# Windowed attention of a hybrid encoder: the key tile beyond each end of a sequence is left out

## The chip, the cores and the metric

The kernel runs on 1 core of one Trainium2 chip. A core has five engines that run side by side and wait for each other by semaphores: TensorE (PE; its weight loads are listed as PEld), VectorE (DVE), ScalarE (ACT), GpSimd (POOL) and SyncE (SP), which here only issues transfers. Transfers run on 16 DMA engines that all queues share. The metric is the device time of one execution in microseconds.

## The reference, cut to what matters

Two token sequences, of 1024 and of 256 tokens, each get 16 meta tokens put in front and pass through one layer: an attention branch and a recurrent branch side by side, then a mixture of 32 experts. The attention is windowed: queries are taken in blocks of 128, and each block sees three blocks of keys, its own and the ones before and after, within a distance of 128, and the 16 meta keys:

```python
kpad = jnp.pad(kr, pad)                       # one block of zeros at either end
def band(n):
    qb = lax.dynamic_slice_in_dim(qr, n * ATTN_BLK, ATTN_BLK, axis=1)
    kb = lax.dynamic_slice_in_dim(kpad, n * ATTN_BLK, 3 * ATTN_BLK, axis=1)
    ...
    valid = (jnp.abs(ki - qi) <= WINDOW) & (ki >= 0) & (ki < s_len)
    s_win = jnp.where(valid, jnp.einsum('bqgrd,bkgd->bgrqk', qb, kb), -jnp.inf)
    s_met = jnp.einsum('bqgrd,bkgd->bgrqk', qb, km)
    return sink_softmax_av(s_win, vb, s_met, vm, sk)
```

For the first block of a sequence the block of keys before it does not exist, and for the last block the one after it: their scores are minus infinity for every query, and their probabilities are zero.

## The kernel before, in words

The two sequences lie one behind the other, 1280 tokens in NB = 10 blocks of 128. Blocks 0 to 7 are the first sequence, 8 and 9 the second. So blocks 0 and 8 are the first of a sequence, 7 and 9 the last.

`project` (from L162) normalises the tokens and makes the keys, values, queries and the recurrent branch feature tile by feature tile (products at L736, the recurrent gates at L758). Its POOL program (L332 to L363) writes zeros into two padding blocks of the key buffer in DRAM (L345 to L347), swaps rows of the keys for their rotation (L351), waits until the values are turned (L353), clears the two padding blocks of the token-major values in SBUF (L354 and L355) and stores the keys to DRAM (L357 to L363). ScalarE (L474) and POOL (L1193) wait for all key stores.

`mix` (from L801) is written as 12 steps, one per block and two to drain; a step is a hand-written order on each engine. Step t does attention for block t, the output product and residual of block t-1, and the router and list entries of block t-2 (`step` at L1383 on TensorE, L1539 on ScalarE, L1860 on VectorE; `run` at L1029 calls them with constant t).

- POOL: `window` (L1183) fetches the 384 keys of a block from DRAM to `k_win`, one of two buffers, one transfer for each of two key groups; `window(t + 1)` is issued at the start of POOL's step t. The 16 meta keys are fetched once into columns 384 to 400 of each buffer. `attn` (L1213) then waits for the exponentials and packs the meta probabilities.
- TensorE: `scores` (L1265) makes 8 heads of 128 x 400 scores, two products each (the high and low parts of the keys, both against the same stationary query parts), in two PSUM buffers that VectorE must have read two heads before. The heads are issued in four pairs among the output products (L1360) of block t-1, turns of block t-2 (L1324) and the router (L1338). `turn_probs` (L1281) turns each head's three 128 x 128 blocks of probabilities (L1288), in four pairs of heads, each behind six output products; a head waits until ScalarE has copied out the head two before. `times_v` (L1300) multiplies with the values: two 512-column instructions for the meta keys (L1307), then 8 heads x 3 key blocks, two instructions each (L1312).
- VectorE: `softmax_max` (L1647) scales, masks and writes one head of scores and takes its maximum (L1661); `rope_q` (L1600) rotates the query of the next block, `split_q` (L1640) splits it in a high and a low part, `attn_output` (L1838) makes the denominators and the attention output of the block before (L1853). The order in a step: attention output, heads 0 to 3, residual, heads 4 to 7, the router's choice of block t-2 (from L1689), rotation of the next query, two residuals, list places, split of the next query, scaled tokens of block t-1. In steps 0 and 1 splits of the output weights (L1637) stand in between.
- ScalarE: `exponentials` (L1439, one instruction per head at L1445), `probs_out` (L1458) copies the turned probabilities, three blocks per head, from PSUM (L1464), `sink_and_rec`, `meta_copy`, `q_split` (L1491).
- SP: swaps rows of the next query for its rotation (`swap_q`, L1066, four transfers at L1068), fetches masks and rotation tables (`tables`, L1058), tokens and weights.

The masks are made on the host (`layouts`, L2617): for a first block the first 128 columns are all minus infinity, for a last block columns 256 to 384.

After step 11, `plan` turns the counts of the router into a table of blocks of tokens per expert; `experts` (from L2006) reads the table and streams expert weights block by block.

Of the kernel before, what the change touches and what calls it, by code (L numbers as in the profile page):

```python
# [30 lines left out]
F32 = mybir.dt.float32  # L31
# [7 lines left out]
P = 128  # L39
D = 1024  # L40
META = 16
# [22 lines left out]
KEYS = WIN + META  # L64

# [96 lines left out]
def project(nc, sem, lasting_sem, block, mk, ps, a, feat, k_pre, v_tok, v_small, ident, eps_t, iota_e, list_dram, h2_dram, k_dram):  # L162
# [103 lines left out]
    v_padded = sem("v_padded")  # L266
    TILES_DONE = 2 * NCH + FTILES * NCH
    K_STORES = 16 * 18
# [63 lines left out]
    def _(pool):  # L332
# [11 lines left out]
        pool.wait_ge(fills, 3)  # L344
        for at in (META, META + P + REAL):  # L345
            pool.dma_start(k_dram[:, :, :, at:at + P].bitcast(F32), zeros[:, 0:4 * P].rearrange("p (g h c) -> p g h c", g=2, h=2)
                           ).then_inc(k_stored, 16)  # L347
# [5 lines left out]
        pool.wait_ge(v_turned, 1)  # L353
        for at in (0, (NB + 1) * P):  # L354
            pool.memset(v_tok[:, at:at + P], 0.0).then_inc(v_padded, 1)  # L355

# [359 lines left out]
    def _(pe):  # L716
# [68 lines left out]
        for k in range(FT):  # L785
            for d in range(2):
# [7 lines left out]
                k_cos_done=(k_cos_done, 1), k_swapped=(k_swapped, 16 * len(ROTATED)), v_out=(v_out, 2), v_padded=(v_padded, 2),  # L794
# [6 lines left out]
def mix(nc, ctx, sem, block, at, ps, a, projected, cleared_later, recycled, q_pre, rec, k_dram, v_tok, v_small, ident, eps_t, iota_e, counts, ix_x,  # L801
# [375 lines left out]
    def _(pool):  # L1177
# [5 lines left out]
        def window(t, s):  # L1183

            if not isinstance(t, int) or t >= 2:
                pool.wait_ge(scored, HEADS * t - HEADS)
                take_waits(pool)
            keys(s, slice(0, WIN), bass.ds(META + t * P, WIN), keys_in[s])
# [24 lines left out]
        def attn(t, s):  # L1213
            if has_next(t):
                window(t + 1, 1 - s)

            pool.wait_ge(exp_done, HEADS * t + HEADS)
            pool.wait_ge(meta_turned, t) if not isinstance(t, int) or t > 0 else None
            take_waits(pool)
            pool.tensor_copy(meta_p[:, :].rearrange("p (h m) -> p h m", m=META), probs[:, :, WIN:KEYS]).then_inc(meta_packed, 1)  # L1220
# [40 lines left out]
    def _(pe):  # L1261
# [3 lines left out]
        def scores(t, s, heads):  # L1265
            if heads[0] == 0:
                pe.wait_ge(q_lo_done, t + 2)
                if isinstance(t, int) and t == 0:
                    pe.wait_ge(projected["proj_out"], projected["PUT"])
                if isinstance(t, int) and t < RING:  # L1270
                    pe.wait_ge(k_meta_in[s], 32)
                pe.wait_ge(keys_in[s], 32 * (t // 2 + 1) if isinstance(t, int) else 16 * (t - s) + 32)
            for h in heads:

                pe.wait_ge(scaled, HEADS * t + h + 1)
                for part in range(2):
                    mm = pe.matmul(ps_sc[h % 2][:, 0:KEYS], q_parts[:, h, :], k_win[s][h // 4][:, part, :],  # L1277
                                   start=(part == 0), stop=(part == 1))
                mm.then_inc(scored, 1)

        def turn_probs(t, heads):  # L1281
            for h in heads:
# [4 lines left out]
                for j in range(3):  # L1287
# [12 lines left out]
        def times_v(t):  # L1300
            if isinstance(t, int) and t == 0:
                pe.wait_ge(v_meta_in, 16 * HEADS)
                pe.wait_ge(*projected["v_out"])
                pe.wait_ge(*projected["v_padded"])
# [3 lines left out]
            for h in range(HEADS):  # L1308
                pe.wait_ge(pt_out, HEADS * t + h + 3)
                for j in range(3):  # L1310
                    last = h == HEADS - 1 and j == 2
# [126 lines left out]
    def _(act):  # L1438
        def exponentials(t, heads):  # L1439
# [4 lines left out]
            for h in heads:  # L1444
                act.activation(probs[:, h, :], probs[:, h, :], ACT.Exp, bias=nmax[:, h:h + 1],  # L1445
# [12 lines left out]
        def probs_out(t, heads):  # L1458
            for h in heads:
# [4 lines left out]
                act.activation(probs_t[:, h, :], ps_t[h % 2][:, 0:WIN], ACT.Copy).then_inc(pt_out, 1)  # L1464
# [125 lines left out]
    def _(dve):  # L1590
# [56 lines left out]
        def softmax_max(t, s, heads, ahead_of_third=None):  # L1647

            for h in heads:
# [11 lines left out]
                dve.tensor_tensor_reduce(probs[:, h, :], ps_sc[h % 2][:, 0:KEYS], mask[s][:, :], HD ** -0.5, sink[:, h:h + 1],  # L1661
# [955 lines left out]
def layouts(i):  # L2617
# [37 lines left out]
    last = (SEQS[0] // P - 1, NB - 1)  # L2655
    first = (0, SEQS[0] // P)
    for b in range(NB):
        masks[b, :, 0:P] = NEG if b in first else np.where(kj >= qi, 0.0, NEG)
        masks[b, :, 2 * P:3 * P] = NEG if b in last else np.where(kj <= qi, 0.0, NEG)
# [39 lines left out]
```

## Time and profile before

| | |
|---|---|
| runs | 1231.37, 1232.2 and 1234.94 us; median 1232.2 us |
| profiled execution, first to last instruction (span) | 1231.0 us; the profile gives no other time for this execution |
| instructions | 21274 |
| TensorE busy | 1177.3 us, 96% of the span |
| VectorE busy | 926.7 us, 75% |
| ScalarE busy | 848.3 us, 69% |
| POOL busy | 253.0 us, 21% |
| mean granted TensorE clock | 0.992 |
| projections and recurrent branch | to about 257 us |
| attention steps 0 to 9 (value products end) | 257 to 529.6 us |
| drain, plan, table of blocks | to about 567 us |
| experts and final norm | to 1231 us |

The profile is one execution, taken by the hardware profiler. Busy time of TensorE is modelled, as its products are pipelined. The chain of waits goes back from the last instruction, at each step to what released it. A line of a view names the line of the kernel, the engine, what is written and read, and, behind a bar or in brackets, the idle time before it with what ended it.

### The profile page before, as it was taken

Reading aid. Unit: us, or ns where it says so; the run is one execution under the profiler, and the core shown is the slowest. Engines: PE = TensorE matmul, PEld = TensorE weight load, DVE = VectorE, ACT = ScalarE, POOL = GpSimd, SP = SyncE. Lnnn points to the kernel's source line nnn. Section 1 sums busy time; section 2 is a strip of 40 time slices with the busy share of each in tenths; the row PEclk is TensorE's granted clock in tenths of the full one; section 3 lists DMA queues with packets and bytes.
Section 4 is the critical chain, followed back from the end, with each engine's and each line's share of the span. In section 5 each row is a group of like instructions: output and inputs, shape, how many; then the busy total and the mean of one; then the engine's idle time right before and its main releaser. Section 6 shows DMA issues by size and latency. Waiting matters only on the chain.

```text
span 1231.0 us, 21274 instructions
## 1 busy us (share of the span) xinstructions
PE 1177.3 (96%) x6126; PEld 1007.2 (82%) x6126; DVE 926.7 (75%) x1214; ACT 848.3 (69%) x1042; POOL 253.0 (21%) x262
## 2 busy tenths in 40 slices
PE   5999999988999999999999999999999999999984
PEld 5999999977888888887788888888888888888872
DVE  5657887457777777758898867555888888888876
ACT  5538889567566666646777756555778777877775
POOL 2130000010111111012333213222322322322420
PEclk9999999999999999999999999999999999999997
DMA  7241110363233323346999987878999999999988
GB/s 289 89 127 40 43 44 29 83 183 95 87 114 93 107 91 91 120 173 246 389 393 404 382 271 254 322 250 315 393 380 384 395 378 377 390 373 373 401 304 334
DMA packets 67687, 295.60 MB, mean 240 GB/s; under 512 B 12469, under 2 KB 23094, under 8 KB 43058
## 3 DMA queue, kind: packets, MB, share of 16 engines
q1 hardware_dynamic: 48626, 252.63, 52.3%
q0 software_dynamic: 19008, 42.31, 14.1%
q8 instruction: 28, 0.46, 0.1%
q14 instruction: 25, 0.20, 0.0%
HBM read 263.98 MB, written 38.14 MB: 245 GB/s over the span
## 4 chain that ended last, share of the span: by engine, by line
PE 65%; DMA 20%; DVE 7%; ACT 4%; issue 3%; SPq 1%; POOL 0%; DVEq 0%; ACTq 0%; POOLq 0%
PE ps L2294 16%; PE ps L736 16%; DMA raw_w_gate<-in_w_gate 15%; PE ps L1360 8%; PE ps L2342 8%; PE ps L1312 4%; PE ps L758 2%; DVE g_lo L2499 2%; PE ps L1277 2%; ACT g_hi L2392 2%; PE ps L1288 2%; DMA raw_w_up<-in_w_up 2%; PE ps L1338 1%; PE ps L2281 1%; DMA z_a<-h_dram,ix_a 1%
## 5 line engine op out<-in xcount | busy, mean ns | idle before, releaser
L2499 DVE TENSOR_TENSOR g_lo<-raw_w_gate,g_hi 128x2048 fp32r<-128x2048 f32 x64 | 145.2, 2289 | 41.3 <-ACT g_hi L2392 41.1
L2499 DVE TENSOR_TENSOR d_lo<-raw_w_down,d_hi 128x2048 fp32r<-128x2048 f32 x62 | 140.5, 2289 | 44.5 <-ACT d_hi L2392 44.5
L2499 DVE TENSOR_TENSOR u_lo<-raw_w_up,u_hi 128x2048 fp32r<-128x2048 f32 x64 | 144.1, 2286 | 5.6 <-ACT u_hi L2392 5.2
L2392 ACT ACTIVATE g_hi<-raw_w_gate 128x2048 fp32r<-128x2048 f32 x64 | 120.9, 1913 | 37.6 <-DMA raw_w_gate<-in_w_gate 32.1
L2392 ACT ACTIVATE u_hi<-raw_w_up 128x2048 fp32r<-128x2048 f32 x64 | 120.9, 1913 | 17.3 <-DMA raw_w_up<-in_w_up 17.1
L736 PE MATMUL ps<-h_hi,w_hi 128*128 128x432 f32 (+2 forms) x368 | 127.6, 347 | 0.6 <-DVE w_lo L581 0.6
L736 PE MATMUL ps<-h_lo,w_hi 128*128 128x432 f32 (+2 forms) x368 | 126.3, 343 | 0.0
L736 PE MATMUL ps<-h_hi,w_lo 128*128 128x432 f32 (+2 forms) x368 | 126.1, 343 | 0.0
L2392 ACT ACTIVATE d_hi<-raw_w_down 128x2048 fp32r<-128x2048 f32 x62 | 116.8, 1909 | 13.5 <-DMA raw_w_down<-in_w_down 13.5
L2342 PE MATMUL ps<-d_hi,hid_hi 128*128 128x512 f32 x272 | 111.5, 410 | 0.7 <-DVE hid_lo L2528 0.7
L2342 PE MATMUL ps<-d_lo,hid_hi 128*128 128x512 f32 x272 | 107.3, 395 | 0.0
L2342 PE MATMUL ps<-d_hi,hid_lo 128*128 128x512 f32 x272 | 107.0, 393 | 0.0
L2222 POOL DMA_INDIRECT h_dram<-y_sb,ix_y x33 | 63.1, 1911 | 99.1 <-ACT y_sb L2428 93.9
L2294 PE MATMUL ps<-g_hi,ex_hi 128*128 128x512 f32 x272 | 75.1, 398 | 4.4 <-DVE ex_lo L2515 3.0
L2196 POOL COPY ix_x<-lists 128x2 int32 x33 | 14.1, 428 | 305.2 <-PE ps L2281 300.4
L2294 PE MATMUL ps<-u_hi,ex_hi 128*128 128x512 f32 x272 | 76.8, 404 | 0.0
L2294 PE MATMUL ps<-g_lo,ex_hi 128*128 128x512 f32 x272 | 74.4, 395 | 0.1
L2294 PE MATMUL ps<-u_lo,ex_hi 128*128 128x512 f32 x272 | 74.4, 395 | 0.0
L2294 PE MATMUL ps<-u_hi,ex_lo 128*128 128x512 f32 x272 | 74.3, 394 | 0.0
L2294 PE MATMUL ps<-g_hi,ex_lo 128*128 128x512 f32 x272 | 74.2, 394 | 0.0
L1661 DVE CUSTOM_DVE_ANT_0 probs<-ps,mask,sink_bc 128x400 f32<-128x400 f32 x80 | 47.5, 631 | 34.7 <-PE ps L1277 33.0
L736 PEld LDWEIGHTS ps<-h_hi,w_hi 128*128 128x128 f32 x368 | 69.9, 190 | 3.0 <-DVE w_lo L581 0.8
(374 smaller groups left out, 2729.9 us busy)
## 6 DMA issues: line engine op xcount, KB each, us to landing
raw_w_gate<-in_w_gate SPq DMA_DIRECT2D x64, 1024.0 KB, 10.8
raw_w_up<-in_w_up SPq DMA_DIRECT2D x64, 1024.0 KB, 12.5
raw_w_down<-in_w_down SPq DMA_DIRECT2D x62, 1024.0 KB, 12.0
k_win<-k_dram POOLq DMA_DIRECT2D x20, 384.0 KB, 5.7
w_raw<-in_w_in SPq DMA_DIRECT2D x14, 512.0 KB, 4.0
xh<-in_x SPq DMA_DIRECT2D x10, 512.0 KB, 3.4
h_dram<-xh SPq DMA_DIRECT2D x10, 512.0 KB, 3.8
u_dram<-u SPq DMA_DIRECT2D x10, 512.0 KB, 4.9
```

The lines of the kernel that those rows point to most:

```text
L736: mm = pe.matmul(ps[:, bank, 0:cols.stop - cols.start], w[s][:, k, :], h[:, k, cols], start=(k == 0 and n == 0), stop=(k == KD - 1 and n = ...
L758: mm = pe.matmul(bank[:, c, 0:n], w[:, g, :], x[:, cols], start=(j == 0), stop=(j == 2))
L1277: mm = pe.matmul(ps_sc[h % 2][:, 0:KEYS], q_parts[:, h, :], k_win[s][h // 4][:, part, :], start=(part == 0), stop=(part == 1))
L1288: mm = pe.transpose(ps_t[h % 2][:, j * P:(j + 1) * P], probs[:, h, j * P:(j + 1) * P], ident[:, :])
L1312: mm = pe.matmul(ps_o[:, h * HD:(h + 1) * HD], probs_t[:, h, j * P:(j + 1) * P], v_tok[:, bass.ds(t * P + j * P + (h // 4) * HD, HD)], sta ...
L1360: mm = pe.matmul(ps_y[i][:, :], x[:, k, :], w[:, k0 + k, half(i)], start=(k == 0 and n == 0), stop=(k == FT - 1 and n == 2))
L1661: dve.tensor_tensor_reduce(probs[:, h, :], ps_sc[h % 2][:, 0:KEYS], mask[s][:, :], HD ** -0.5, sink[:, h:h + 1], ALU.add, ALU.max, smax[:, ...
L2222: pool.indirect_dma_start(h2_dram, bass.IndirectOffsetOnAxis(ap=ix_y[:, 0:1], axis=0), y[:, :], None, compute_op=ALU.add).then_inc(y_added ...
L2294: mm = pe.matmul(ps[:, :], xs[:, c * KG + k, :], w[c][:, k * FE:(k + 1) * FE], start=(c == 0 and k == 0 and j == 0), stop=(c == 1 and k == ...
L2342: mm = pe.matmul(ps_y[:, i, :], h[:, c * KDN + k, :], w[c][:, cols], start=(c == 0 and k == 0 and j == 0), stop=(c == 1 and k == KDN - 1 a ...
L2392: act.activation(hi[c][:, :], raw[c][:, :], ACT.Copy).then_inc(hi_done, 1)
L2499: dve.tensor_tensor(lo[c][:, :], raw[c][:, :], hi[c][:, :].bitcast(F32), ALU.subtract).then_inc(lo_done, 1)
```

## The change

In steps 0 and 8 the first of the three key blocks is left out, in steps 7 and 9 the last. Scores, the scaled and masked scores, and exponentials cover 272 instead of 400 columns there; turns, copies and value products two instead of three blocks; the key fetch 256 instead of 384 keys. So that the columns stay next to each other in steps 7 and 9, the meta keys and probabilities sit in columns 256 to 272 there: step 7 fetches the meta keys once more, behind its 256 keys, into the buffer that step 9 uses too. The padding blocks of keys and values are no longer cleared, and the waits for that go. The other six steps are as before.

```diff
+FIRSTS = (0, SEQS[0] // P)
+LASTS = (SEQS[0] // P - 1, NB - 1)
+def chunks(t):
+    return range(1 if t in FIRSTS else 0, 2 if t in LASTS else 3)
+def meta_at(t):
+    return 2 * P if t in LASTS else WIN
+def key_cols(t):
+    return slice(chunks(t)[0] * P, meta_at(t) + META)
...
-    K_STORES = 16 * 18
+    K_STORES = 16 * 16
...
-        pool.wait_ge(fills, 3)
-        for at in (META, META + P + REAL):
-            pool.dma_start(k_dram[:, :, :, at:at + P].bitcast(F32), zeros[:, 0:4 * P].rearrange("p (g h c) -> p g h c", g=2, h=2)
-                           ).then_inc(k_stored, 16)
...
-        pool.wait_ge(v_turned, 1)
-        for at in (0, (NB + 1) * P):
-            pool.memset(v_tok[:, at:at + P], 0.0).then_inc(v_padded, 1)
...
-            keys(s, slice(0, WIN), bass.ds(META + t * P, WIN), keys_in[s])
+            lo, hi = chunks(t)[0] * P, (chunks(t)[-1] + 1) * P
+            keys(s, slice(lo, hi), slice(META + t * P + lo, META + t * P + hi), keys_in[s])
+            if t == LASTS[0]:
+                keys(s, slice(meta_at(t), meta_at(t) + META), slice(0, META), keys_in[s])
...
-            pool.tensor_copy(meta_p[:, :].rearrange("p (h m) -> p h m", m=META), probs[:, :, WIN:KEYS]).then_inc(meta_packed, 1)
+            pool.tensor_copy(meta_p[:, :].rearrange("p (h m) -> p h m", m=META), probs[:, :, meta_at(t):meta_at(t) + META]
+                             ).then_inc(meta_packed, 1)
...
-                pe.wait_ge(keys_in[s], 32 * (t // 2 + 1) if isinstance(t, int) else 16 * (t - s) + 32)
+                pe.wait_ge(keys_in[s], 32 * (t // 2 + 1) + (32 if t >= LASTS[0] and s == LASTS[0] % RING else 0))
...
-                    mm = pe.matmul(ps_sc[h % 2][:, 0:KEYS], q_parts[:, h, :], k_win[s][h // 4][:, part, :],
+                    mm = pe.matmul(ps_sc[h % 2][:, key_cols(t)], q_parts[:, h, :], k_win[s][h // 4][:, part, key_cols(t)],
...
-                for j in range(3):
+                for j in chunks(t):
                     mm = pe.transpose(ps_t[h % 2][:, j * P:(j + 1) * P], probs[:, h, j * P:(j + 1) * P], ident[:, :])
...
-                pe.wait_ge(*projected["v_padded"])
...
-                for j in range(3):
-                    last = h == HEADS - 1 and j == 2
+                for j in chunks(t):
+                    last = h == HEADS - 1 and j == chunks(t)[-1]
...
-                act.activation(probs[:, h, :], probs[:, h, :], ACT.Exp, bias=nmax[:, h:h + 1],
+                act.activation(probs[:, h, key_cols(t)], probs[:, h, key_cols(t)], ACT.Exp, bias=nmax[:, h:h + 1],
...
-                act.activation(probs_t[:, h, :], ps_t[h % 2][:, 0:WIN], ACT.Copy).then_inc(pt_out, 1)
+                keys = slice(chunks(t)[0] * P, (chunks(t)[-1] + 1) * P)
+                act.activation(probs_t[:, h, keys], ps_t[h % 2][:, keys], ACT.Copy).then_inc(pt_out, 1)
...
-                dve.tensor_tensor_reduce(probs[:, h, :], ps_sc[h % 2][:, 0:KEYS], mask[s][:, :], HD ** -0.5, sink[:, h:h + 1],
+                dve.tensor_tensor_reduce(probs[:, h, key_cols(t)], ps_sc[h % 2][:, key_cols(t)], mask[s][:, key_cols(t)], HD ** -0.5, sink[:, h:h + 1],
...
-        masks[b, :, 0:P] = NEG if b in first else np.where(kj >= qi, 0.0, NEG)
-        masks[b, :, 2 * P:3 * P] = NEG if b in last else np.where(kj <= qi, 0.0, NEG)
+        masks[b, :, 0:P] = np.where(kj >= qi, 0.0, NEG)
+        if b not in LASTS:
+            masks[b, :, 2 * P:3 * P] = np.where(kj <= qi, 0.0, NEG)
```

## Rows read from the trace of the kernel before

**Rows 1.** Stretches of steps 0, 8 and 9: length; busy by engine; clock; DMA share.
```profile
core 0: us, PE busy (x) PEld busy (x) DVE busy (x) ACT busy (x) POOL busy (x), PEclk, DMA share, GB/s
254.00:278.08 24.08, 19.45 (x126) 15.68 (x125) 17.11 (x35) 20.51 (x42) 6.07 (x16) 1.00 0.74 209
...
473.70:501.69 27.99, 27.77 (x177) 24.03 (x176) 21.31 (x68) 18.12 (x46) 2.75 (x6) 1.00 0.34 104
501.69:529.64 27.95, 27.70 (x177) 24.04 (x176) 18.04 (x63) 16.87 (x44) 3.02 (x7) 1.00 0.39 150
```

**Rows 2.** Chain of waits, one gate pass and step 8: start us, us, what.
```profile
104.83 3.60 PE ps L758 x18
...
474.49 2.79 PE ps L1360 x12
477.27 0.72 PE ps L1277 x4
...
481.63 0.39 PE ps L1277 x2
...
482.89 1.19 PE ps L1277 x4
...
485.79 1.47 PE ps L1360 x6
487.26 0.66 PE ps L1288 x6
...
489.37 0.89 PE ps L1288 x6
...
495.30 1.10 PE ps L1307 x2
496.39 5.30 PE ps L1312 x48
```

**Rows 3.** Order of time, VectorE and POOL in step 7: start us, us, instruction, [idle before].
```profile
449.84 0.63 DVE L1661 CUSTOM_DVE_ANT_0 probs<-ps,mask,sink_bc 128x400 f32<-128x400 f32 x1 [2.18 <-PE ps L1277]
...
457.97 0.24 DVE L1689 SCALAR_TENSOR_TENSOR logits<-ps,rstd_h,rbias_bc 128x40 f32<-128x40 f32 x1
...
466.18 0.75 DVE L1750 SCALAR_TENSOR_TENSOR xh<-ps,rstd_a,xh 128x512 f32<-128x512 f32 x1 [0.43 <-DVE xh L1750]
...
470.01 1.39 DVE L1643 TENSOR_TENSOR q_parts<-q_cos,q_parts 64x512 fp32r<-64x512 f32 x2
...
473.80 0.69 DVE L1853 TENSOR_TENSOR attn_o<-ps,rden 128x512 f32<-128x512 f32 x1 [0.57 <-PE ps L1312]
...
472.34 1.53 POOL L1181 DMA_DIRECT2D k_win<-k_dram  x2
```

**Rows 4.** Order of time around step 0, SP's queue and VectorE.
```profile
249.89 1.39 SPq L1068 DMA_DIRECT2D q_alt<-feat  x2
252.63 0.69 DVE L1609 TENSOR_TENSOR q_sin<-q_alt,sin_q 128x512 f32<-128x512 f32 x1 [3.74 <-DMA q_alt<-feat]
...
266.01 2.99 SPq L1068 DMA_DIRECT2D q_alt<-feat  x4
...
270.94 0.69 DVE L1609 TENSOR_TENSOR q_sin<-q_alt,sin_q 128x512 f32<-128x512 f32 x1
...
277.91 1.28 DVE L1637 SCALAR_TENSOR_TENSOR wo_lo<-wo_raw,g_out,wo_hi 128x1024 fp32r<-128x1024 f32 x1
```

**Rows 5.** Line L758 between 100 and 110 us: durations in ns, forms.
```profile
L758 PE MATMUL ps<-xc_hi,gates_hi x6: 297/390/396, 104.7 to 107.9; 128*128 128x512 f32 x4, 128*128 128x292 f32 x2
```

**Rows 6.** Transfers between 240 and 310 us: issues, KB each, median us to landing.
```profile
k_win<-k_dram POOLq DMA_DIRECT2D x6, 384.0 KB, 4.4
...
k_win<-k_dram POOLq DMA_DIRECT2D x2, 16.0 KB, 6.7
```

**Rows 7.** Chain of waits ahead of the experts: start us, us, what.
```profile
564.50 2.37 DMA table<-table_dram
```

**Rows 8.** Stretches in the drain, columns as in rows 1.
```profile
554.00:556.00 2.00, 1.13 (x8) 0.99 (x9) 1.44 (x9) 2.00 (x2) 0.00 (x0) 1.00 0.99 352
556.00:558.00 2.00, 2.00 (x12) 2.00 (x11) 1.69 (x11) 2.00 (x2) 0.94 (x1) 0.54 0.40 164
```

More of the change, by code:

```diff
@@ L265, in project @@
     v_out = sem("v_out")
-    v_padded = sem("v_padded")
     TILES_DONE = 2 * NCH + FTILES * NCH
-    K_STORES = 16 * 18
+    K_STORES = 16 * 16
     def rows(t):
@@ L793, in project @@
                 gates_dead=(gates_done, 1 + 4 * (FT - 1)), rec_done=(rec_done, 2 + 2 * FT), k_stored=(k_stored, K_STORES),
-                k_cos_done=(k_cos_done, 1), k_swapped=(k_swapped, 16 * len(ROTATED)), v_out=(v_out, 2), v_padded=(v_padded, 2),
+                k_cos_done=(k_cos_done, 1), k_swapped=(k_swapped, 16 * len(ROTATED)), v_out=(v_out, 2),
                 w_split=(w_lo_done, done(FTILES - 2)), last_outputs=last_outputs)
@@ L2654, in layouts @@
     qi, kj = np.arange(P)[:, None], np.arange(P)[None, :]
-    last = (SEQS[0] // P - 1, NB - 1)
-    first = (0, SEQS[0] // P)
     for b in range(NB):
-        masks[b, :, 0:P] = NEG if b in first else np.where(kj >= qi, 0.0, NEG)
-        masks[b, :, 2 * P:3 * P] = NEG if b in last else np.where(kj <= qi, 0.0, NEG)
+        masks[b, :, 0:P] = np.where(kj >= qi, 0.0, NEG)
+        if b not in LASTS:
+            masks[b, :, 2 * P:3 * P] = np.where(kj <= qi, 0.0, NEG)
     before = (np.arange(P)[:, None] < np.arange(P)[None, :]).astype(f)
```

## The prediction

> **What bounds the kernel now.** Four views, in this order. First the table of stretches, cut where the value products of one attention step end: from the third step on a step takes 27.9 to 28.0 us and TensorE is busy for 27.7 of it at granted clock 1.00, VectorE for 21.3 (18.0 in the last step), ScalarE for 18; only the first stretch has TensorE busy for 19.5 of 24.1 [rows 1]. Second the chain of waits: in such a step it stays on TensorE nearly throughout, so what TensorE does not do there comes off the end. It leaves TensorE for about 0.9 us, where score 6 waits for VectorE to read score 4, and for a hair ahead of the second pair of turns [rows 2]. Third VectorE's order of time, to see what comes next if TensorE is quicker: VectorE runs without a hole from the router's logits to the softmax denominators but for 0.43 us, and waits 0.57 us for the value products [rows 3]. Fourth the first step by itself: here ScalarE and VectorE set the time [rows 4]. The steps with a masked tile are 0, 7, 8 and 9, and step t uses the stretch numbered t in that table.
>
> **The three steps 7, 8 and 9.** TensorE's part per step:
>
> Scores: 16 products shrink from 400 to 272 columns. Four of 400 take 0.72, so 0.18 each; twelve of 512 take 2.79, so 0.23 each [rows 2]. No row has 272, but a gate pass has twelve of 512 and six of 292 columns [rows 5] and takes 3.60 [rows 2]: the six cost 3.60 - 2.79 = 0.81, or 0.135 each. From 512 to 292 columns that is 0.44 ns a column, from 400 to 292 0.42; 128 columns are 0.053 to 0.057. I take 0.05: 16 x 0.05 = 0.8 us. The bounds are 0 (a floor already at 400, against which the 292 row speaks) and 0.9. VectorE's eight readings of 0.63 [rows 3] shorten too, by 0 to 128/400 of that, 0.20; I take two thirds, 0.13, since some part of an instruction stays whatever its width, so the wait inside the scores does not grow.
> The Trainium skill, page "TensorE: Matmul & The Clock Gate", section "Back-to-back issue gap", gives 81 ns at 128 columns and 131 ns at 512 for streams of a weight load and a product. By it 128 columns would be worth 17 ns, the scores 0.27 us a step, and the sum 1.6 us less. The trace disagrees: 512 columns take 0.23 us here.
>
> Turns: 8 of 24 transposes go, at 0.66/6 = 0.11: 0.88 us. The second pair's six take 0.89 after a short wait for ScalarE [rows 2]; ScalarE's copies and its eight exponentials before them are a third narrower too, so ScalarE gets there earlier and I count 0.25 for this lag, 0.89 against 0.66, as gone; its bounds are 0 and that.
> Value products: 32 of 48 instructions stay, at 5.30/48 = 0.11: 16 x 0.11 = 1.77 us [rows 2]. A bound from below is nothing, if what was loaded were not the limit, but the row counts loads and products together.
>
> Sum on TensorE: 0.8 + 0.88 + 0.25 + 1.77 = 3.7 us a step.
>
> **What is late next.** From the end of the router's products (485.79) to the end of the step (501.69) TensorE takes 15.9; with turns, lag and value products shorter 13.0. VectorE's chain from the logits to the split queries that the next step's scores need (457.97 to 470.01 + 1.39, less the 0.43 hole) is 13.0 long and starts some 0.15 later [rows 3]; none of it is shortened by the change. So steps 7 and 8 end 13.15 after the router, not 13.0: TensorE waits 0.15 for the queries, and the steps save 0.8 + 15.9 - 13.15 = 3.55. Behind this VectorE reaches the attention output about 2 us after TensorE has begun the next step (it is ready at 473.80 - 0.57, so 14.8 after the logits without the hole); it used to stand idle 2.18 us a little later for the third score [rows 3], and that hides it; with that cover gone the excess would stop scores 2 and 3. Step 9 has no next query to prepare (VectorE 18.0 us [rows 1]), so it saves the full 3.7. Together 3.55 + 3.55 + 3.7 = 10.8 us.
>
> **Step 0.** The same removals there would be worth about 4 us on the path through ScalarE: sixteen instructions (eight exponentials, eight copies) that I shorten like VectorE's, 16 x 0.13 = 2.1, then 1.77 of value products. But step 1 begins on VectorE: rotating and splitting step 1's query, then splits of the output weights up to 279.2, one behind the other [rows 4]. The rotation needs the four query swaps that SP issues from 266.01 to 269.00, whose time nothing here moves. In the swap before, the last issue ended at 251.28 and the rotation, which waited for it, began at 252.63, 1.35 later [rows 4]. So the rotation of step 1 can begin at 269.00 + 1.35 = 270.35 instead of 270.94: 0.6 us, and VectorE's line up to the scores of step 1 moves by just that. Bounds: 0, if the swaps landed just then, and 1.6, since twelve of ScalarE's sixteen (12 x 0.13) lie ahead of the gate squares that VectorE sums before it rotates. I take 0.6, since the earlier swap is the nearest row. The rest of the 4 us becomes TensorE standing idle for the weight splits in step 1.
>
> **What costs nothing.** The key fetch shrinks by a third. It is issued about 29 us before its use (472.34, for the scores at 501.69) [rows 3] and lands in 4.4 [rows 6]. Step 7 gets two more fetches of 16 columns on POOL's queue, 16 KB in 6.7 us [rows 6]; POOL's next work is a copy that waits for the step's exponentials, so nobody is kept behind them. Cover gone, they cost 6.7 us; the cover is over 20. Two zero fills and two clears ahead of the key stores go from POOL's queue; the first key fetch that reads those stores is far behind them, so this is worth nothing. Masks and tables on SP's queue stay.
>
> **After attention.** The experts' weights are fetched once the table of blocks has landed at 566.9 [rows 7]; the table follows the last step's routing, and the chain has no other start, so the gain is carried whole to the end.
>
> **Sum.** 10.8 + 0.6 = 11.4 us. The profiled execution's span is 1231.0; the trace tells nothing around it. 1231.0 - 11.4 = 1219.6. The median run is 1232.2, 1.2 above that span, so 1220.8.
>
> **Rivals.**
> VectorE closes the ring in steps 7 to 9. For: its hole ahead of the attention output is 0.57 us. Against: it waits 2.18 us for scores within the same step [rows 3]. Then a step gains only what VectorE does less (8 x 0.13 = 1.0) and the scores' 0.8: 3 x 1.8 + 0.6 = 6.0, 1226.2. Chance 0.15.
> Step 0 gives all of its 4 us: 10.8 + 4 = 14.8 us, 1217.4. Against: the swaps. Chance 0.08.
> The clock drops at step 0. TensorE idles near 2 us before step 1's output products. In the trace the granted clock was 1.00 to 556 and then 0.54, most of a 2 us stretch at 1.2 GHz instead of 2.4, after TensorE had been busy for 1.13 of the 2 us before [rows 8]; two such stretches cost about 1.8 us: 1222.6. Chance 0.06.
> Beside that row, the Trainium skill's page "TensorE: Matmul & The Clock Gate", Part 1, says that the full clock is what activity earns and idleness takes away, which speaks against making the turns fewer; the trace agrees at 556.
> The gain is given back before the experts, if the weight stream waits for something other than the table: 1232. Against: the chain goes through the table. Chance 0.04.
> Slower: products of 272 columns leave the quick path. The products with meta values (plain fp32) take 1.10/2 = 0.55 per 512-column instruction, two instructions each [rows 2]; at that rate a 272-column score would be 2 x 0.29 = 0.58 instead of 0.18, 16 x 0.40 = 6.4 us more a step against 2.9 saved: 3 x 3.5 = 10.5, less step 0's 0.6, 1242. It decides once a product takes over 0.18 + 2.9/16 = 0.36. Against: the 292-column price. Chance 0.03.
>
> **How the numbers follow.** The forecast keeps 0.64. Only the last two rivals are not faster: faster 0.93, same 0.04, slower 0.03, with 0.3% (3.7 us) as what a measurement of this kernel can tell. The range runs from just under the rival of 1217.4 to the one of 1226.2: 1216.5 to 1226.5.
>
> **What would show it.** Steps 7 and 8 at 24.3 to 24.5 us, step 9 at 24.2; score products at 0.13; 32 value instructions in 3.5; VectorE without a wait for value products in steps 8 and 9, and a short wait of score products for split queries; the first stretch about 4 shorter, but the second about 3 longer, TensorE idle in it. I am wrong if steps 7 to 9 stay above 25.5, if step 1 begins its softmax more than 1.6 earlier, or if the stretch after 529.6 grows.

## The result, and the profile after

Five runs of the changed kernel took 1219.4, 1219.74, 1220.13, 1224.75 and 1224.99 us, median 1220.13. The runs of before beside them have a median of 1232.2 (1229.57 to 1234.94); the ratio is 0.9904, 95% interval 0.9881 to 0.9928. The profiled execution of after took 1220.13 us with a span of 1218.3, against 1231.0 before. The kernel is faster by 12.1 us, 1.0%. Runs of one kernel scatter by several microseconds, so the single terms of the sum are read from the traces. One run of the experiments (of the value products alone) took 1948.17 us at a mean granted clock of 0.557 and is left out of every figure below.

The stretches of steps 7, 8 and 9 after, cut where the chain of waits begins the next step's work (columns as in [rows 1]):

```profile
core 0: us, PE busy (x) PEld busy (x) DVE busy (x) ACT busy (x) POOL busy (x), PEclk, DMA share, GB/s
444.53:468.65 24.12, 23.89 (x153) 20.61 (x151) 18.51 (x65) 16.44 (x46) 1.72 (x5) 1.00 0.34 104
468.65:493.01 24.36, 24.12 (x152) 20.85 (x152) 20.22 (x69) 16.44 (x46) 4.12 (x8) 1.00 0.35 104
493.01:517.16 24.15, 24.09 (x152) 20.97 (x153) 18.64 (x67) 15.18 (x44) 3.08 (x6) 1.00 0.39 153
```

They answer to [rows 1]: 27.99 and 27.95 became 24.36 and 24.15, and TensorE is still busy for nearly all of it. From the start of step 7's scores to the last value product it is 84.06 us before (445.57 to 529.63) and 72.82 after (444.34 to 517.16): 11.24 us less. From one step's first score product to the next one's, steps 7 and 8 save 3.63 and 3.64 us, and step 9, to its last value product, 3.97.

The chain of waits through steps 7 to 9 and ahead of the experts (start, us, what):

```profile
453.91 1.71 PE ps L1346 x16
455.62 1.47 PE ps L1368 x6
457.09 0.44 PE ps L1297 x4
457.53 1.39 PE ps L1368 x6
...
463.37 0.74 DVE xh L1759
467.20 0.52 DVE q_parts L1652
467.90 0.70 DVE q_parts L1652
468.65 0.78 PE ps L1286 x4
469.42 2.75 PE ps L1368 x12
472.18 0.51 PE ps L1286 x4
...
513.64 3.52 PE ps L1320 x32
...
552.16 2.38 DMA table<-table_dram
```

Against [rows 2]: four score products take 0.51 instead of 0.72 (0.13 each), a pair of turns is four in 0.44, thirty-two value products take 3.52. What is new is VectorE in the middle: from 463.37 to 468.60 the chain lies on its instructions, up to the split queries, and only then do step 8's scores begin. The same place in order of time, VectorE, TensorE and POOL (start, us, instruction, idle before):

```profile
468.65 0.78 PE L1286 MATMUL ps<-k_win,q_parts 128*128 128x272 f32 x4 [0.17 <-DVE q_parts L1652]
...
470.45 0.69 DVE L1862 TENSOR_TENSOR attn_o<-ps,rden 128x512 f32<-128x512 f32 x1
471.06 0.49 DVE L1670 CUSTOM_DVE_ANT_0 probs<-ps,mask,sink_bc 128x272 f32<-128x272 f32 x1
...
472.62 0.50 DVE L1670 CUSTOM_DVE_ANT_0 probs<-ps,mask,sink_bc 128x272 f32<-128x272 f32 x1 [0.64 <-PE ps L1286]
...
469.52 1.54 POOL L1186 DMA_DIRECT2D k_win<-k_dram  x2
```

Against [rows 3]: the 0.57 us for which VectorE waited for value products ahead of the attention output is gone, TensorE waits 0.17 for the queries instead, and the wait for the third score, 2.18 before in step 7 and 2.23 in step 8, is 0.64 in step 8. VectorE is late there, and has used up 1.6 us of its slack ahead of the third score. The table of blocks lands at 554.54 instead of 566.87 [rows 7], 12.33 earlier.

Step 0 in order of time, SP's queue, VectorE and TensorE. First what [rows 4] does not have of before, the first score products of steps 0 and 2 and the eight value copies on SP's queue:

```profile
257.66 0.96 PE L1277 MATMUL ps<-k_win,q_parts 128*128 128x400 f32 x4 [0.67 <-issue]
258.41 5.98 SPq L1101 DMA_DIRECT2D v_meta<-v_small  x8
...
305.72 0.97 PE L1277 MATMUL ps<-k_win,q_parts 128*128 128x400 f32 x4
```

After:

```profile
257.40 0.74 PE L1286 MATMUL ps<-k_win,q_parts 128*128 128x272 f32 x4 [0.67 <-issue]
258.15 5.50 SPq L1106 DMA_DIRECT2D v_meta<-v_small  x8
265.34 2.99 SPq L1073 DMA_DIRECT2D q_alt<-feat  x4
...
269.68 0.69 DVE L1618 TENSOR_TENSOR q_sin<-q_alt,sin_q 128x512 f32<-128x512 f32 x1 [0.64 <-DMA q_alt<-feat]
...
276.65 1.28 DVE L1646 SCALAR_TENSOR_TENSOR wo_lo<-wo_raw,g_out,wo_hi 128x1024 fp32r<-128x1024 f32 x1
...
276.38 0.50 PE L1368 MATMUL ps<-wo_hi,rec_hi 128*128 128x512 f32 x1 [1.31 <-DVE wo_lo L1646]
...
304.44 0.97 PE L1286 MATMUL ps<-k_win,q_parts 128*128 128x400 f32 x4
```

Against [rows 4]: the rotation now waits for the swaps and starts 1.35 us after the end of their last issue (268.33 to 269.68). TensorE, early for step 1, waits 1.31 us for a weight split. From first score product to first score product, step 0 is 3.53 us shorter (20.23 before, 16.70 after) and step 1 is 2.51 longer (27.83, 30.34). Steps 0 and 1 together are 48.06 us before (257.66 to 305.72) and 47.04 after (257.40 to 304.44).

The granted clock in step 0 after, in stretches of 2 us:

```profile
258.00:260.00 2.00, 1.16 (x7) 0.68 (x5) 1.57 (x7) 1.98 (x3) 1.84 (x10) 1.00 0.81 283
260.00:262.00 2.00, 1.67 (x8) 1.20 (x9) 1.58 (x8) 1.99 (x6) 1.33 (x2) 0.94 1.15 395
262.00:264.00 2.00, 1.80 (x9) 1.36 (x8) 1.83 (x7) 2.00 (x9) 0.00 (x0) 0.50 1.44 336
264.00:266.00 2.00, 2.00 (x15) 2.00 (x14) 1.81 (x2) 2.00 (x10) 0.21 (x1) 0.70 1.10 284
266.00:268.00 2.00, 1.40 (x13) 1.11 (x13) 1.21 (x2) 1.82 (x6) 0.07 (x1) 1.00 0.35 80
```

Before, it is 1.00 in step 0. After, it falls to 0.50, the 1.2 GHz level, shortly before 262; TensorE had been busy for 1.16 and 1.67 of 2 us in the two stretches up to there. Here it costs nothing that lasts: the rotation still had to wait 0.64 us for the swaps, and with the clock kept up (the first version with idle products, below) the two steps take 47.02, no less. What such a fall does a few microseconds later, the experiments show.

### The profile page after: what moved, and what is told of

Its sections match the earlier page's. It is cut to its first block, busy times and chain, and to the rows that moved or that the text cites. A ratio compares the mean times of both kernels' runs of the same rounds, so it can differ in the third digit from the quotient of the medians.

```text
span 1218.3 us, 21079 instructions
## 1 busy us (share of the span) xinstructions
PE 1162.6 (95%) x6030; PEld 993.7 (82%) x6030; DVE 922.0 (76%) x1214; ACT 841.3 (69%) x1042; POOL 249.1 (20%) x260
## 3 DMA queue, kind: packets, MB, share of 16 engines
HBM read 262.97 MB, written 37.62 MB: 247 GB/s over the span
## 4 chain that ended last, share of the span: by engine, by line
PE 63%; DMA 20%; DVE 8%; ACT 3%; issue 3%; SPq 2%; POOL 0%; DVEq 0%; ACTq 0%; POOLq 0%
PE ps L2303 16%; PE ps L741 16%; DMA raw_w_gate<-in_w_gate 15%; PE ps L1368 8%; PE ps L2351 8%; PE ps L1320 3%; PE ps L763 2%; DVE g_lo L2508 2%; ACT g_hi L2401 2%; PE ps L1286 2%; DMA raw_w_up<-in_w_up 2%; PE ps L1297 2%; PE ps L1346 1%; PE ps L2290 1%; DMA z_a<-h_dram,ix_a 1%
## 5 line engine op out<-in xcount | busy, mean ns | idle before, releaser
L741 PEld LDWEIGHTS ps<-h_hi,w_lo 128*128 128x128 f32 x368 | 69.6, 189 | 2.5
## 6 DMA issues: line engine op xcount, KB each, us to landing
raw_w_gate<-in_w_gate SPq DMA_DIRECT2D x64, 1024.0 KB, 10.8
```

The costliest lines, as they stand in the source:

```text
L741: mm = pe.matmul(ps[:, bank, 0:cols.stop - cols.start], w[s][:, k, :], h[:, k, cols], start=(k == 0 and n == 0), stop=(k == KD - 1 and n = ...
```

## The experiments

The first four split the change by steps and by parts. **Steps 7 to 9 alone**: the changed kernel, with step 0 on all three chunks again, and the zero fills and clears back for it.

```diff
-FIRSTS = (0, SEQS[0] // P)
+FIRSTS = (SEQS[0] // P,)
...
-        masks[b, :, 0:P] = np.where(kj >= qi, 0.0, NEG)
+        masks[b, :, 0:P] = NEG if b == 0 else np.where(kj >= qi, 0.0, NEG)
```

> The change in steps 7, 8 and 9 alone; step 0 and POOL's zero fills and clears stay as before. Theory (TensorE's own work sets these steps, VectorE caps 7 and 8): the three steps take 24.1, 24.4 and 24.15 us as in the changed kernel, step 0 as before; 11.3 us under the kernel before, about 1221, so ratio 0.991. Rival (a good part of the whole gain comes from step 0 or from the work taken off POOL's queue early on): under 9 us, ratio 0.993 or more.

Measured: 1219.86 us (1218.39 to 1223.56), ratio 0.991 (0.988 to 0.9941). In the trace steps 7 and 8 take 24.34 and 24.36, from 445.55 to the last value product at 518.44 it is 72.89, as in the whole change; steps 0 and 1 are 48.06, as before. So the three steps bring all of the gain that the runs can tell.

**Step 0 alone**:

```diff
-FIRSTS = (0, SEQS[0] // P)
-LASTS = (SEQS[0] // P - 1, NB - 1)
+FIRSTS = (0,)
+LASTS = (NB,)
```

> The change in step 0 alone; 7, 8 and 9 and the zero fills and clears as before. Theory (the swaps of step 1's query, on SP's queue, cap step 0): VectorE's rotation waits for them and begins 1.35 us after the last swap's issue ends; 0.6 us from this, with SP's own shifts up to 1.3, ratio 0.999 to 1.000. Rival (the removed work of step 0 counts in full): 4 us, ratio 0.997.

Measured: 1233.51 us (1230.1 to 1238.43), ratio 1.0008 (0.9983 to 1.0032): nothing. Yet the rotation starts 12.41 us after step 0's first score, against 13.28 before. In the profiled execution steps 0 and 1 together are not shorter but longer, 50.58 us, and its rows tell why: two stretches of 6 us (columns as in [rows 1]), then the value products of step 0 and what stands around them:

```profile
270.00:276.00 6.00, 6.00 (x24) 4.97 (x24) 4.58 (x6) 4.64 (x6) 1.43 (x2) 0.50 0.88 270
276.00:282.00 6.00, 6.00 (x22) 5.50 (x22) 5.57 (x11) 5.44 (x8) 0.00 (x0) 0.50 0.74 228
```

```profile
269.66 2.05 PE L1324 MATMUL ps<-v_meta,meta_t 128*128 128x512 f32 x2 [0.58 <-ACT meta_t L1489]
271.49 6.93 PE L1329 MATMUL ps<-v_tok,probs_t 128*128 128x64 f32 x32
278.18 1.68 PE L1294 MATMUL ps<-k_win,q_parts 128*128 128x400 f32 x4
```

The clock stands at the 1.2 GHz level from 270 to 282, over value products that then take 6.93 us (3.68 in after, in the same column) and over step 1's first output products. TensorE had been busy for 5.32 of the 8 us from 262 to 270 before it fell.

**Value products alone**, then **value products and turns**, both put into the kernel before; scores, softmax and key fetches keep their full width (the second also narrows ScalarE's copies).

```diff
-                for j in range(3):
-                    last = h == HEADS - 1 and j == 2
+                for j in chunks(t):
+                    last = h == HEADS - 1 and j == chunks(t)[-1]
```

> Only the value products of the masked tile are left out, in steps 0, 7, 8 and 9. Theory: 16 instructions of 0.11 us, 1.77 us in each of steps 7, 8 and 9, since VectorE's chain to the split query still ends before TensorE (13.15 against 14.1 after the router): steps of 26.2 us, nothing in step 0; 5.3 us in all, ratio 0.9957. Rival (VectorE closes the ring at once, its hole ahead of the attention output being 0.57 us): steps of 27.4 us, 1.7 us in all, ratio 0.9986.

> Value products, turns and ScalarE's copies of the masked tile are left out, in steps 0, 7, 8 and 9; scores, masks and exponentials stay 400 columns wide. Theory: after the router 13.15 us in steps 7 and 8 (VectorE's chain, 0.15 over TensorE's 13.0) and 13.0 in step 9 instead of 15.9: steps of 25.2, 25.2 and 25.1 us, 8.4 us, and 0.4 in step 0; 8.8 us in all, ratio 0.9929. The rest to the changed kernel, 1.0 us a step, is then what scores and softmax bring. Rival (turns lie behind ScalarE's copies or weight loads and bring nothing): as with the value products alone, 5.3 us.

Measured: 1228.73 us (nine runs), ratio 0.9954 (0.9929 to 0.9979), and 1227.12, ratio 0.9953 (0.9934 to 0.9972). The first is as expected, the second is not. Step 7 takes 26.16 and 25.38 us, against 27.94 before and 24.31 with everything: the value products bring 1.78, the turns 0.78, and scores and exponentials the last 1.07. With value products and turns, steps 7, 8 and 9 take 25.38, 25.43 and 25.52, each 0.2 to 0.4 more than expected, 0.8 in all. What else the runs lack is again in step 0: steps 0 and 1 take 50.90 and 50.43 in these two traces, with the granted clock at 0.50 from about 272 to 282.

**A longer tail.** Four small VectorE instructions ahead of the split of the next queries in steps 7 to 9 of the changed kernel, to see who closes the step.

```diff
+            if t in (7, 8, 9):
+                for _ in range(4):
+                    dve.tensor_copy(place_i[:, :], place2[:, :]).then_inc(cleared, 1)
+                    n_slow[0] += 1
+                    dve.wait_ge(cleared, n_slow[0])
             if t is not None and has_next(t):
                 split_q(t + 1)
```

> The changed kernel with four more copies of 2 elements, each waiting for the one before, on VectorE ahead of the split of the next query in steps 7, 8 and 9: about 0.2 us each, 0.8 us a step. Theory (VectorE's chain sets the end of steps 7 and 8, TensorE that of step 9): steps 7 and 8 grow by 0.8 each to 24.9 and 25.2, step 9 stays at 24.15; 1.6 us in all. Rival (TensorE sets all three): under 0.4 in all. Other rival (VectorE sets all three): 2.4.

Measured: step 7 took 25.02 us and step 8 25.05, 0.71 and 0.69 more than in the changed kernel; step 9 24.20, 0.05 more. The rows at the end of steps 7 and 8 show the wait (VectorE's added work, then TensorE's score products and their idle time):

```profile
467.27 0.77 DVE L1914 CAST place_i<-place 128x2 int32<-128x2 f32 x4
468.08 1.39 DVE L1653 TENSOR_TENSOR q_parts<-q_cos,q_parts 64x512 fp32r<-64x512 f32 x2
```

```profile
469.52 0.65 PE L1287 MATMUL ps<-k_win,q_parts 128*128 128x272 f32 x3 [0.87 <-DVE q_parts L1653]
...
494.57 0.77 PE L1287 MATMUL ps<-k_win,q_parts 128*128 128x272 f32 x4 [0.86 <-DVE q_parts L1653]
```

The added 0.7 us goes through in full where a next query is split, and not at all in step 9. VectorE sets the end of steps 7 and 8, TensorE that of step 9. (The median of the runs, 1225.82, lies 5.7 above that of after, more than 1.45; two of its five runs have a mean granted clock of 0.984 and 0.985.)

**Swaps later, swaps earlier.** In the changed kernel SP issues three constants ahead of step 1's query swaps instead of behind them; or the eight small value copies go from SP's queue to POOL's, which lets the swaps go out sooner.

```diff
-        sp.wait_ge(q_sin_done, 1)
-        swap_q(1)
         for dst, src in ((router[:, :, :], a["router"]), (rbias[:, :], a["rbias"][0].partition_broadcast(P)),
                          (before[:, :], a["before"])):
             sp.dma_start(dst, src).then_inc(consts_in, 16)
+        sp.wait_ge(q_sin_done, 1)
+        swap_q(1)
```

> The changed kernel with three loads of constants (0.44, 0.43 and 0.43 us of issue) moved ahead of the four swaps of step 1's query on SP's queue. Theory (the swaps set when step 1 begins on VectorE): the rotation begins 1.3 to 1.5 us later and still 1.35 after the last swap's issue, and steps 1 to 9 and the end move by as much: ratio to the kernel before 0.9916 if the changed kernel is at 0.9904. Rival (ScalarE's exponentials and copies set it, the swaps are hidden): nothing moves.

> The changed kernel with the eight loads of the values of the meta tokens on POOL's queue instead of SP's, ahead of the tables and swaps of step 1, so that these are issued some 5.5 us earlier. Theory: VectorE's rotation no longer waits for the swaps (0.64 us in the changed kernel); it begins when the sum of squares is done, 0.6 us earlier, and then VectorE's splits of the output weights set the start of step 1: 0.6 us under the changed kernel, not more. Rival (only the swaps stand between step 0 and its 4 us): 2 to 3 us under it.

Swaps later, SP's queue and VectorE:

```profile
267.38 2.97 SPq L1073 DMA_DIRECT2D q_alt<-feat  x4
...
271.70 0.69 DVE L1618 TENSOR_TENSOR q_sin<-q_alt,sin_q 128x512 f32<-128x512 f32 x1 [2.52 <-DMA q_alt<-feat]
```

Swaps earlier:

```profile
259.59 2.90 SPq L1073 DMA_DIRECT2D q_alt<-feat  x4
...
268.69 0.69 DVE L1618 TENSOR_TENSOR q_sin<-q_alt,sin_q 128x512 f32<-128x512 f32 x1
```

Counted from step 0's first score product (at 257.64 and 257.24 in these two), and against the changed kernel, the swaps are issued 1.80 us later, 0.44 of it because the eight value copies ahead of them take 5.94 us instead of 5.50, and the rotation comes 1.78 later, again 1.35 behind the end of the last issue. Issued 5.59 earlier, they bring it forward by 0.83 only: it no longer waits for them, and the work of ScalarE and VectorE ahead of it is the limit. Both had the clock at 0.50 from about 270 to 282, which hides this in the runs: 1225.18 us, ratio 0.9923 (0.9893 to 0.9954), and 1223.08, ratio 0.9903 (0.9867 to 0.994).

One number ties these traces together. With the clock up from 268 on, step 2 begins a fixed time after step 1's rotation: 34.78 us before (270.94 to 305.72), 34.76 after (269.68 to 304.44), 34.78 with steps 7 to 9 alone, 34.77 with the longer tail (where the clock was down from 270 to 273 only). With the clock down from about 270 to 282 it is 38.17 (step 0 alone), 37.62, 37.59 (the two of value products and turns), 36.58 and 38.95 us (swaps later, earlier): 1.8 to 4.2 us lost.

**Idle products.** So the question became whether TensorE's waits in step 0 bring the clock down. First, two idle products (128 columns of a unit matrix by itself, a result that nobody reads; the kernel before has eight of them in step 0 already) ahead of each of the scores of heads 2 to 7 in step 0 of the changed kernel:

```diff
             for h in heads:
 
+                if t == 0 and h >= 2:
+                    idle_products(pe, 2, ps_y[0])
                 pe.wait_ge(scaled, HEADS * t + h + 1)
```

> The changed kernel with two idle products (128 columns) ahead of each of the scores of heads 2 to 7 in step 0. In the changed kernel the granted clock is 0.94, 0.50 and 0.70 in the stretches from 260 to 266 us. Theory (the clock falls because TensorE does little in step 0, but it costs nothing, since the swaps set the start of step 1): the clock stays at 1.00, the rotation begins at the same time, the time is that of the changed kernel within 0.5 us. Rival (the lower clock takes back part of step 0's gain): 1 to 2 us less.

Measured: 1221.73 us (1218.18 to 1224.53), ratio 0.9903 (0.9866 to 0.994). The profiled execution has 1.00 throughout steps 0 and 1, which take 47.02 together; but the two slower of its four runs have mean clocks of 0.987 and 0.989. These products fill the waits up to 262; the ones after it stay open.

Then idle products in all waits from step 0's scores to step 1's first output product, four kernels on one chip: in the changed kernel, in the kernel before, with steps 7 to 9 alone, and with the swaps earlier.

```diff
+            if isinstance(t, int) and t == 0:
+                idle_products(pe, 4, ps_y[0])
             pe.wait_ge(ssq_r_out, t + 1)
...
             if isinstance(b, int) and b == 0 and i == 0:
+                if part == 0:
+                    idle_products(pe, 9, ps_y[0])
                 pe.wait_ge(wo_lo_done, FT * part + ks[-1] + 1)
```

> The changed kernel with idle products put into every wait of TensorE between the first scores of step 0 and the first output product of step 1 (two ahead of heads 2 to 7, six, one and four around the last turns and the meta turn, nine ahead of the first output product). Clock theory (the 3.4 us by which steps 0 and 1 are longer in some runs are the granted clock at 0.50 from about 269 to 283 us, after TensorE had waited in step 0): the profile shows 1.00 from 256 to 284 us, steps 0 and 1 together take 46.8 to 47.3 us, and no run of this kernel is more than 3 us above its lowest: median 1218 to 1220. Rival (what falls in step 0 is not set by TensorE's waits there): the clock falls in steps 0 and 1 as often as before, runs stand in two groups about 5 us apart, and the median is 1219 to 1225.

> The kernel before with the same idle products. Clock theory: its runs lose their upper group (about 1236 to 1240), the median is 1230 to 1232, steps 0 and 1 together take 48.0 to 48.4 us. Rival: two groups remain, median 1231 to 1237.

> Steps 7 to 9 short, step 0 with all three chunks, and the same idle products. If step 0's part of the change is worth its 1.0 us once the clock stays up: steps 0 and 1 together 48.0 to 48.4 us, median 0.7 to 1.4 above that of the changed kernel with idle products. Rival (step 0's part is worth nothing): median within 0.3 of it.

> The changed kernel with the small value copies moved from SyncE's queue to GpSimd's (so that the swaps start earlier) and the same idle products. If only the landing of the swaps sets the start of step 1: rotation 1.0 us earlier than in the changed kernel with idle products, steps 0 and 1 together 45.8 to 46.4 us, median 0.7 to 1.3 below it. Rival (the end of step 0's value products on TensorE, 274.10 in the changed kernel, sets it just as well): steps 0 and 1 together within 0.4 of 47.0, same median.

Measured in the changed kernel: 1219.6 us (1217.15 to 1221.31, six runs), ratio 0.988 (0.9847 to 0.9913). Steps 0 and 1 take 47.05, step 2 begins 34.77 after the rotation, and the clock stays up; the stretches of 6 us as for step 0 alone:

```profile
270.00:276.00 6.00, 6.00 (x50) 5.76 (x49) 4.62 (x7) 5.54 (x7) 1.43 (x2) 1.00 0.99 298
276.00:282.00 6.00, 6.00 (x35) 5.19 (x34) 5.89 (x16) 5.74 (x9) 0.00 (x0) 1.00 0.59 177
```

Its runs reach 4.2 us above the lowest, not the 3 that were expected, but none has a mean clock under 0.989. The kernel before with idle products: 1234.86 us (1231.38 to 1238.75, twelve runs), ratio 1.0003 (0.9981 to 1.0025). None of the twelve has a mean clock under 0.989, while four of the seventeen plain runs beside them stand at 0.986 and 1239.14 to 1240.32 us. With the idle products the group of low clocks is gone, as the clock theory has it: none of the thirty runs of the four kernels has 0.987 or less. But the times of before with idle products still reach 1238.75 us at a mean clock of 0.991, the median is not 1230 to 1232, and steps 0 and 1 take 50.27, not 48.0 to 48.4. The miss has its own cause, in the rows of step 1 (before with idle products; the first line is the nine of them, two passes each):

```profile
277.78 2.17 PE L1250 MATMUL ps<-ident 128*128 128x128 f32 x18
279.71 0.48 PE L1368 MATMUL ps<-wo_hi,rec_hi 128*128 128x512 f32 x1
```

Nine idle products take 1.93 us, 0.21 each and so twice a turn's 0.11, and with step 0 at full length TensorE has no wait there to put them in: step 2 begins 36.84 after the rotation, 2.06 late. The same holds for steps 7 to 9 alone (36.86, and 50.29 for the two steps; 1223.36 us, ratio 0.9916), so more than half of its distance of 3.8 us from the changed kernel is the price of the idle products, and it settles nothing about step 0's worth. With the swaps earlier (1220.66 us, ratio 0.9885, 0.9853 to 0.9917) the rotation comes 11.68 us after step 0's first score instead of 12.28, but step 2 begins 35.12 after it: 46.80 for the two steps against 47.05. That is more than the theory's 45.8 to 46.4 and within the rival's 0.4 of 47.0, but the rival's reason (the end of step 0's value products) is not what the rows of step 1 show. They show the nine idle products, and right behind them the first output product:

```profile
275.07 2.17 PE L1259 MATMUL ps<-ident 128*128 128x128 f32 x18
276.99 0.48 PE L1376 MATMUL ps<-wo_hi,rec_hi 128*128 128x512 f32 x1
```

It starts 8.26 behind the rotation; before it is 7.77, with step 2 still on time. So 0.35 of the 0.60 went to the idle products. None of the versions of the changed kernel is distinguishable from it by its interval, so nothing here beats it.

## Why the prediction was right, and where it was not

The forecast was 1220.8 us, the median is 1220.13, and the sum came close term by term: 11.4 us forecast, 12.26 measured in the traces (11.24 in steps 7 to 9, 1.02 in steps 0 and 1). It was made against the span: 1231.0 - 11.4 = 1219.6, measured 1218.3. That the median lies as near as 0.7 us is in part luck. The five runs scatter over 5.6 us, and the 1.2 us added to the span took the median run for the profiled one, where the runs of after are 1.8 to 1.9 us longer than their own spans; this made up for half of the gain that the sum had missed.

- **Scores, 0.8 a step.** From the first score product of step 7 to its first router product it is 10.35 us before and 9.41 after (445.57 to 455.92, 444.34 to 453.75): 0.94. A 272-column product costs 0.50/4 = 0.125, so 16 save 0.055 each, 0.88; I had rounded the estimate of 0.053 to 0.057 down to 0.05. VectorE's readings shrank from 0.63 to 0.49, 0.14 where I took 0.13.
- **"No row has 272"** was wrong. The projections of the kernel before have such products: in its chain of waits twenty-four of 272 columns take 3.02 us, 0.126 each (the first row is that of the chain, the second one of its products):

```profile
25.97 3.02 PE ps L736 x24
26.19 0.29 PE L736 MATMUL ps<-h_hi,w_hi 128*128 128x272 f32 x1
```

This row would have given the price directly, and would have left the slow-path rival, at 0.58 a product, almost nothing. (From 20.92 to 23.19 the same products start every 0.227 us, although the stretches of that trace have the granted clock at 1.00 there: the prediction's "1.00 to 556" is what the view says, and the products of the first 24 us do not fit it.)

- **Turns 0.88 and lag 0.25.** The lag goes, but with the narrower scores and exponentials, not with the turns: turns with narrower copies alone bring 0.78, and there the second pair of step 7 still waits 0.19 us for ScalarE; in the changed kernel none of its four pairs waits.
- **Value products 1.77.** Alone they bring 1.78; thirty-two take 3.52.
- **VectorE closes steps 7 and 8 at 13.15 behind the router's end.** Measured 13.03 and 13.02, with the split queries as the last wait; the longer tail shows that this is the limit there and not in step 9. VectorE's chain takes 12.92 us (455.67 to 468.59 in step 7), begins 0.05 behind the router's end, and TensorE starts 0.06 behind it. The three steps gave 11.24 where I had 10.8: 0.08 and 0.09 more in steps 7 and 8, 0.27 in step 9. In steps 7 and 8 the 0.14 of the scores and the 0.12 of VectorE's chain are set off by 0.18 that the sum had too much: the 15.9 us of before ran to the end of the value products (501.69), but step 9's first score product starts at 501.51. In step 9 the scores gave 0.12 more than the 0.8, and what follows the router 0.15 more than the 2.9 (15.90 before, 12.85 after).
- **What costs nothing.** No score product of the changed kernel waits for keys: the only idle time ahead of them ends with VectorE or with issue. The four fetches for step 7, the two of meta keys among them, are issued at 414.89, 29 us ahead of its scores, and land in 5.6 to 5.8 us; the two for step 9, issued at 469.52, have over 23 us.
- **Step 0, 0.6.** The mechanism held: the landing of the swaps, 1.35 us behind their last issue, sets the rotation in every trace where it had to wait for them. The size did not: steps 0 and 1 are 1.02 shorter. The step that failed is "whose time nothing here moves". Counted from step 0's first score, the swaps were issued after 8.35 us before and 7.94 after; the eight value copies ahead of them on SP's queue took 5.98 and 5.50 us. It is no effect of the change, since with step 0 changed they also took 5.68 and 5.94 (step 0 alone, swaps later), and with step 0 as before 5.58 (steps 7 to 9 alone). So 0.4 of the 1.0 us is scatter of SP's queue, and the prediction had read its time from a trace in which the copies took longer than in any other. The upper bound of 1.6 was about right: with the swaps out of the way the rotation begins 11.68 after step 0's first score with idle products and 11.45 without, 1.60 and 1.83 earlier than before. The first step came out 3.53 us shorter and the second 2.51 longer, where about 4 and 3 had been named as signs. The runs do not show this term: the rest of the program from the table's landing to the end took 664.1 us before, 663.8 after and 660.6 with steps 7 to 9 alone, which scatters by more.
- **The rival "the clock drops at step 0"** had a chance of 0.06, and its price was off. That it is step 0 was right. But the reason given was TensorE's idling ahead of step 1's output products, and the falls come earlier, at about 270, before step 0's value products or among them; in the changed kernel TensorE does wait 1.31 us ahead of those output products, at 1.00. And I took it for something that only the changed kernel could do, at 1.8 us. Of the ten traces without idle products in all the waits, five have the clock down from about 270 to 282, and it costs 1.8 to 4.2 us between the rotation and step 2. The kernel before does it too, by its runs: of twenty-six in one comparison, seventeen lie at 1229.76 to 1232.78 us with mean clocks of 0.990 and up, nine at 1236.06 to 1239.79 with 0.986 or 0.987. The two runs of after at 1224.75 and 1224.99, both at 0.984, look like that group. Two things stay open. The groups of before are some 6 us apart, more than the 1.8 to 4.2, and no trace shows such a run of before, so where the rest lies is not known. All five traces with the long fall have step 0 shortened in part or in whole, so the change may make the fall more frequent: a mean clock of 0.987 or less in sixteen of thirty-one runs of the five kernels that have step 0 short throughout and no idle products put in (two of five of after among them), against thirteen of the thirty-seven runs of before beside four of these (seventeen of fifty-four with those beside the last four experiments). These counts do not settle it. If it is so, that can eat the microsecond that step 0 gives.

The Trainium skill, page "TensorE: Matmul & The Clock Gate", section "HAM oscillation", says that idle gaps throw the array back to half clock, and that each return is paid again. The traces agree on the price (value products 6.93 against 3.68 us). But here the clock also fell after short waits: from 262 to 270 in the kernel with step 0 alone none is longer than 1.0 us.

The other three rivals did not come. VectorE did not close the ring (it still waits 0.64 us for the third score), step 0 did not give its 4 us (TensorE waits 1.31 us for the splits instead), and nothing was given back: the table landed 12.33 us earlier and the span is 12.7 shorter.

## What to carry to other kernels

Cost a removal from the chain of the engine that ends the step, then walk the next engine's chain to the same end, and let the longer one cap the gain; here that gave each step to 0.3 us. Where one engine paces a stage and another has stood idle in it, ask which wait now ends last before counting anything (at step 0 a step 3.5 us shorter gave 1.0; by the start of the rotation, without the wait for four transfers it would have given 1.6 to 1.8). Before a term is bounded from afar, search the whole trace for the very shape, also in stages that have nothing to do with the change.

## What the runs showed of the hardware that was not expected

- TensorE's granted clock fell to 0.50 for about 12 us in some executions of the same stage and not in others, after 8 us in which TensorE had been busy for 5.32 us with no wait over 1.0 us (step 0 alone). The trace of before has 5.63 in the same 8 us and no fall, that of the value products alone 5.83 and a fall, so the busy share of that stretch does not tell the two apart. Idle products in those waits kept the clock at 1.00 through steps 0 and 1 in all four traces that had them.
- A swap of rows by four small transfers was ready 1.35 to 1.36 us after the end of the last issue in each of the six traces where its reader was waiting, whenever it was issued (264.51 to 267.38).
- fp32r products cost 0.125 us at 272 columns, 0.18 at 400 and 0.23 at 512, 0.43 ns more a column from 272 to 400 and 0.47 from 400 to 512.
